# A hybrid decoder layer on one core: attention probabilities turned by VectorE blocks and a trip through DRAM

## What is computed

```python
scores = jnp.einsum('bnqchd,bnkchd->bnchqk', qb, kb,
                    preferred_element_type=jnp.float32) * (hd ** -0.5)
...
m = jnp.max(scores, axis=-1, keepdims=True)
e = jnp.exp(scores - m)
den = jnp.sum(e, axis=-1)
o = jnp.einsum('bnchqk,bnkchd->bnqchd', e, vb.astype(jnp.float32))
```

## Time and profile before

| | |
|---|---|
| time, three runs | 1344.31, 1344.43, 1344.99 us |
| span of the profiled execution | 1342.2 us |
| TensorE busy | 1331.9 us, 99% of the span |
| VectorE, ScalarE, GpSimd busy | 781.2, 507.8, 531.0 us |
| attention steps | about 328 to 850 us |

### The profile page before, as it was taken

One profiled execution on the slowest core, in us unless ns is written; L12 is line 12 of the kernel. 1 busy time (PEld: TensorE's weight loads), 2 busy tenths in 40 slices (PEclk: granted clock), 3 DMA queues, 4 the chain that ended last, 5 costly groups with the idle time before them and its releaser, 6 DMA issues.

```text
span 1342.2 us, 17647 instructions
## 1 busy us (share of the span) xinstructions
PE 1331.9 (99%) x6262; PEld 1104.3 (82%) x6262; DVE 781.2 (58%) x1253; ACT 507.8 (38%) x1282; POOL 531.0 (40%) x500
## 2 busy tenths in 40 slices
PE   9999999999999999999999999999999999999998
PEld 6887888888888888888888888888888888888887
DVE  6799887842779666565665752148512566134323
ACT  7455646542434444344443688311200011223100
POOL 6975424404458334041340632342067317044020
PEclk9999999999999999999999999999999999999999
DMA  6232312322203032120320332376279644122111
GB/s 240 79 102 87 109 56 79 110 100 72 75 12 84 24 92 64 31 83 22 97 58 30 114 98 88 100 237 220 94 275 412 198 126 157 55 79 63 40 47 47
DMA packets 84823, 139.51 MB, mean 104 GB/s; under 512 B 10464, under 2 KB 41472, under 8 KB 84736
## 3 DMA queue, kind: packets, MB, share of 16 engines
q10 hardware_dynamic: 40288, 75.82, 16.0%
q1 hardware_dynamic: 44448, 62.56, 15.6%
HBM read 108.84 MB, written 29.51 MB: 103 GB/s over the span
## 4 chain that ended last, share of the span: by engine, by line
PE 92%; DVE 5%; issue 1%; ACT 1%; DMA 0%; POOL 0%; SPq 0%; POOLq 0%; DVEq 0%; ACTq 0%
PE bank L1275 28%; PE bank L1280 28%; PE bank L1279 28%; PE bank L1432 2%; PE bank L1412 2%; PE bank L1399 1%; PE bank L1421 1%; DVE xc L1012 1%; PE bank L1525 1%; PE bank L1320 0%; DMA gain_mix<-in_gain_mix 0%; ACT L750 0%; DVE ibuf L1039 0%; DVE qkr L1116 0%; DVE ibuf L1028 0%
## 5 line engine op out<-in xcount | busy, mean ns | idle before, releaser
L549 POOL TENSOR_TENSOR ring<-raw,ring 128x512 fp32r<-128x512 f32 x221 | 310.5, 1405 | 727.1 <-PE bank L1280 642.8
L1275 PE MATMUL bank<-hn,ring 128*128 128x512 f32 x640 | 251.8, 393 | 1.4 <-DVE sgbuf L1000 1.2
L1280 PE MATMUL bank<-hn,ring 128*128 128x512 f32 x640 | 249.4, 390 | 0.0
L1279 PE MATMUL bank<-hn,ring 128*128 128x512 f32 x640 | 249.2, 389 | 0.0
L1275 PE MATMUL bank<-ring,hn 128*128 128x512 f32 x576 | 232.6, 404 | 0.2 <-POOL ring L549 0.2
L1280 PE MATMUL bank<-ring,hn 128*128 128x512 f32 x576 | 225.8, 392 | 0.0
L1279 PE MATMUL bank<-ring,hn 128*128 128x512 f32 x576 | 225.2, 391 | 0.0
L553 POOL TENSOR_SCALAR ring<-raw 128x512 fp32r<-128x512 f32 x221 | 183.5, 830 | 7.9 <-DMA raw<-in_w_rnn_s 7.8
L1275 PEld LDWEIGHTS bank<-hn,ring 128*128 128x128 f32 x640 | 120.2, 188 | 26.7 <-DVE sgbuf L1000 1.6
L1280 PEld LDWEIGHTS bank<-hn,ring 128*128 128x128 f32 x640 | 120.1, 188 | 25.3
L1279 PEld LDWEIGHTS bank<-hn,ring 128*128 128x128 f32 x640 | 120.3, 188 | 24.0
(11 more groups left out here) (181 smaller groups left out, 2153.7 us busy)
## 6 DMA issues: line engine op xcount, KB each, us to landing
raw<-in_w_tail_s SPq DMA_DIRECT2D x104, 256.0 KB, 2.7
g_in<-gate_dram ACTq DMA_DIRECT2D x48, 256.0 KB, 4.4
raw<-in_w_rnn_s SPq DMA_DIRECT2D x45, 256.0 KB, 2.6
raw<-in_w_qkv_s SPq DMA_DIRECT2D x48, 192.0 KB, 2.5
gate_dram<-g_out ACTq DMA_DIRECT2D x32, 256.0 KB, 2.1
raw<-in_w_qkv_s SPq DMA_DIRECT2D x48, 128.0 KB, 2.2
o_dram<-o_buf ACTq DMA_DIRECT2D x48, 128.0 KB, 1.8
o_in<-o_dram ACTq DMA_DIRECT2D x12, 512.0 KB, 3.5
```

The lines of the kernel that those rows point to most:

```text
L549: nc.gpsimd.tensor_tensor(ring[:, ring_slot(p), 1], raw[:, p % RAW], ring[:, ring_slot(p), 0].bitcast(F32), ALU.subtract).then_inc(w_ready, 1)
L1275: ins = T.matmul(out, lhs[0], rhs[0], start=first, stop=False)
L1279: T.matmul(out, lhs[0], rhs[1], start=False, stop=False)
L1280: return T.matmul(out, lhs[1], rhs[0], start=False, stop=last)
```

## The change

TensorE no longer turns the exponentials. VectorE turns each 32x32 block of the tile within itself, in place in `scores`. ScalarE's queue then writes the tile to a DRAM scratch tensor with four DMAs, one for each 32 partitions, in pieces of 32 numbers (128 B), and in the next step reads it back with one DMA, laid out so that the blocks stand in their turned places in `probsT`. Bank 6 and ScalarE's copy out of it are no longer used. The read takes a step of its own, so the product with the values comes one step later (lag 7), and there are 103 steps instead of 102.

```diff
-LAG_T, LAG_QK, LAG_ET, LAG_PV = 2, 4, 5, 6
+LAG_T, LAG_QK, LAG_ET, LAG_IN, LAG_PV = 2, 4, 5, 6, 7
...
+        turn_dram = nc.dram_tensor("turn_dram", (4, 2 * QUADS, QUAD, QUADS, QUAD), F32, kind="Internal").ap()
...
@@ ScalarE, attention(A), behind the copy to qkT
+                g = A - LAG_ET
+                if 0 <= g < TILES:
+                    b0 = 0 if has_prev(g // (HEADS * NT), g % NT) else QUADS
+                    act.wait_ge(et_done, g + 1)
+                    if g >= 4:
+                        act.wait_ge(probsT_in[g % 2], 16 * ((g - 4) // 2 + 1))
+                    for i in range(QUADS):
+                        act.dma_start(turn_dram[g % 4, b0:, :, i].rearrange("b i j -> i b j"),
+                                      scores[i * QUAD:(i + 1) * QUAD, g % 2, b0 * QUAD:].rearrange(
+                                          "p (b j) -> p b j", j=QUAD)).then_inc(et_out[g % 2], 16)
                 g = A - LAG_QK
...
@@ ScalarE, behind the exponential
-                g = A - LAG_ET
+                g = A - LAG_IN
                 if 0 <= g < TILES:
-                    act.wait_ge(et_done, g + 1)
+                    b0 = 0 if has_prev(g // (HEADS * NT), g % NT) else QUADS
+                    act.wait_ge(et_out[g % 2], 16 * QUADS * (g // 2 + 1))
                     if g >= 2:
                         act.wait_ge(pv_done, g - 1)
-                    nc.scalar.activation(probsT[:, g % 2, c0:], bank[6][:, c0:2 * P], ACT.Copy).then_inc(etc_done, 1)
+                    act.dma_start(probsT[:, g % 2, b0 * QUAD:].rearrange("p (b q) -> p b q", q=P),
+                                  turn_dram[g % 4, b0:].rearrange("(b c) i a j -> (c i) b (a j)", c=QUADS)
+                                  ).then_inc(probsT_in[g % 2], 16)
...
@@ VectorE, attention(A)
+                g = A - LAG_ET
+                if 0 <= g < TILES:
+                    c0 = 0 if has_prev(g // (HEADS * NT), g % NT) else P
+                    dve.wait_ge(exp_done, g + 1)
+                    V.transpose(scores[:, g % 2, c0:], scores[:, g % 2, c0:]).then_inc(et_done, 1)
                 g = A - LAG_QK
...
                     if g >= 2:
-                        dve.wait_ge(et_done, g - 1)
+                        dve.wait_ge(et_out[g % 2], 16 * QUADS * (g // 2))
...
@@ TensorE, attention(A)
-                g = A - LAG_ET
-                if 0 <= g < TILES:
-                    pe.wait_ge(exp_done, g + 1)
-                    if g >= 1:
-                        pe.wait_ge(etc_done, g)
-                    for b in ((0, 1) if has_prev(grp, tile) else (1,)):
-                        ins = T.transpose(bank[6][:, b * P:(b + 1) * P], scores[:, g % 2, b * P:(b + 1) * P], ident[:])
-                    ins.then_inc(et_done, 1)
...
-                    pe.wait_ge(etc_done, g + 1)
+                    pe.wait_ge(probsT_in[g % 2], 16 * (g // 2 + 1))
```

More of the change, by code:

```diff
@@ L35 @@
 CLASSES = (1, 4, 8)
+QUAD = 32
+QUADS = P // QUAD
 OFF_Z_RNN = RNN
@@ L402, in build_layer @@
         et_done = sem("et_done")
-        etc_done = sem("etc_done")
+        et_out = [sem("et_out0"), sem("et_out1")]
+        probsT_in = [sem("probsT_in0"), sem("probsT_in1")]
         pv_done = sem("pv_done")
@@ L752, in attention @@
                                          ).then_inc(exp_done, 1)
-                g = A - LAG_ET
+                g = A - LAG_IN
                 if 0 <= g < TILES:
-                    grp, tile = g // (HEADS * NT), g % NT
-                    c0 = 0 if has_prev(grp, tile) else P
-                    act.wait_ge(et_done, g + 1)
+                    b0 = 0 if has_prev(g // (HEADS * NT), g % NT) else QUADS
+                    act.wait_ge(et_out[g % 2], 16 * QUADS * (g // 2 + 1))
                     if g >= 2:
                         act.wait_ge(pv_done, g - 1)
-                    nc.scalar.activation(probsT[:, g % 2, c0:], bank[6][:, c0:2 * P], ACT.Copy).then_inc(etc_done, 1)
+                    act.dma_start(probsT[:, g % 2, b0 * QUAD:].rearrange("p (b q) -> p b q", q=P),
+                                  turn_dram[g % 4, b0:].rearrange("(b c) i a j -> (c i) b (a j)", c=QUADS)
+                                  ).then_inc(probsT_in[g % 2], 16)
                 g = A - LAG_PV
```

## The result

The changed kernel takes 1382.12 us (median of 4 runs, 1378.71 to 1384.34) against 1344.71 us (4 runs, 1344.31 to 1345.31): 1.0276 times the time before, with an interval of [1.0261, 1.0291]. 1345.0 with a range of 1338 to 1376 was predicted: the time is 37 us above the value and outside the range. The profiled span is 1376.9 us, 34.7 more than before.

The account below looks back on a forecast made before the run. TensorE, busy for 99% of the span, was taken to bound the kernel. -14.4 + 1.5 + 13.4 = +0.5 us on the profiled 1342.2, plus 2.2 from span to median, gave 1345 us, range 1338 to 1376.

Parts of the forecast that it names:

- The transposes removed: Qkv stage: 121 transposes at 0.11 us leave TensorE, 13.3 us, plus a 1.1 us wait: 14.4 us gained.
- The block transpose on VectorE: Every tile's step: 0.26 us for one block, 0.39 to 0.51 for two, hidden behind VectorE's idle time, costed at nothing.
- The price of an issue: ScalarE's queue: each write holds it 0.385 us (one-block tile) or 0.42 us (two-block tile), set between traced issues by piece count.
- The first rival: Issues are dear: at 0.50 us each the gate stage gets 7 us more, 1352, up to 1360 at 0.6; chance 0.25.
- So it is a microsecond early, and nothing waits: Qkv stage, two-block step: the read tile lands at 4.9 us, TensorE wants it at 5.9, so no wait.
- The chunk's end: Qkv stage: read 2 us later at chunk ends; three right before a step cost TensorE 0.5 us each, 1.5 us.
- The gate stage: ScalarE nearly full: 3.6 us more for each four steps, 14.4 over 16 steps, less about 1: 13.4 us lost.
- the three write steps behind these 16 have less work on ScalarE and cost nothing: Gate stage, after the last copy to `qkT`: ScalarE has less to do, so these steps add nothing.
- Late landing: Many small pieces make reads land 4 us after issue, TensorE waits 38 us in the steps: 1383; chance 0.12.
- ScalarE keeps up: Gate stage: an issue holds the queue only 0.28 us, so its loss is 8 us less 1: 1338.5; chance 0.20.
- The clock: Gate stage: waits make TensorE's clock fall, matmuls take twice as long, 66 us more, 14 hidden: about 1397; chance 0.03.
- The rule on short pieces: Writes in 128 B pieces: under 512 B DMA misses its rate; twice the traced 2 us would give Late landing's sum.

Follow-up runs that it names:

- e14: Changed kernel, writes put behind the exponential; round trip only for tiles 26 to 77 less those read at chunk ends, others turned on TensorE: 1338.02 us.
- e11: Changed kernel, writes behind the exponential, read ahead of it, two output banks; last 18 tiles turned on TensorE: 1345.77 us.
- e7: Changed kernel with each of the four writes cut in two (eight of 16 partitions, same 128 B pieces): 1473.79 us.
- e8: Changed kernel with four writes, but each row sent as one piece of 512 or 1,024 B, blocks left in wrong places: 1378.45 us.
- e4: Changed kernel, but the value product reads `ident` instead of the turned probabilities and doesn't wait for the read to land: 1364.82 us.
- e10: Changed kernel with the round trip for the first 78 tiles; the last 18 turned on TensorE and copied by ScalarE as before: 1355.09 us.
- e12: As e11, but the first 26 tiles too turned on TensorE; round trip only for tiles 26 to 77: 1340.65 us.

## Why the prediction was wrong

**The transposes removed: right.** 13.3 us at 0.11 each were taken off the qkv stage. In e14, where 43 tiles make the round trip and 62 transposes are gone (6.8 us), the time is 6.3 us shorter, with 0.8 us of waits for `o_buf`.

**The block transpose on VectorE: right in its price, wrong in "costs nothing".** It takes 0.31 us for one block and 0.43 for two, inside the bounds. But in the sentence "it hides behind that idle time" the average over 422 us stood for every step. In the two stretches in which GpSimd permutes, VectorE's rotations take three times as long (1.2 to 1.3 us against 0.42) and the transpose comes 1 to 5 us later in its step. What is behind it was not asked either: ScalarE's queue stands at the writes. That these stretches are what the first 26 tiles lose 5.1 us by is read from the trace and from e11 to e14, which take those tiles out as a whole; moving the permutation itself wasn't tried.

**The price of an issue: mis-sized.** 0.385 and 0.42 us were taken; the median is 0.455, and behind the first the issues in a row start 0.47 to 0.50 apart on either queue. The two of `cossin` were the right row, and the eight small ones the wrong one. "128 pieces, between these ends" assumed that pieces set the price; e7 and e8 show that between 32 and 256 pieces they hardly do. Why those eight came at 0.36 each stays open. The first rival had the price right, and its time (1352 to 1360) wrong, because it charged it to the gate stage alone.

**"So it is a microsecond early, and nothing waits": the step that failed in the qkv stage.** For a plain two-block step it held: of the 76 value products up to the gate stage 15 waited, nearly all at chunk ends or where GpSimd permutes. The landing times of the earlier trace rows spread from 1.8 to 4.4 us, and one number was taken for all steps. The median read lands in 2.1 us (2.2 was taken), but at chunk ends, beside weight loads and the bias load, most take 3 to 4. The chunk's end was seen, and priced 1.5 us; of the 19.4 us of waits up to 763 us, 13.6 lie there, 4.5 where GpSimd permutes, and one of 1.3 behind a read whose issue alone took 1.43 us. Summed from start to start of TensorE's matmuls in the qkv stage of the two traces, 13.1 us of transposes and 1.8 us of waits went, and 22.5 us of waits, 1.8 us in products whose weights were no longer loaded ahead, and 1.7 us of large matmuls, nearly all at the lower clock, came: +11.1, against +10.5 measured.

**The gate stage: the right mechanism, 10.8 us short.** Up to step 97 it lost 16.9 us where 13.4 were forecast. By the sum four steps were to take 19.57 + 3.6 = 23.2 us (the 22.5 named as a sign does not follow from that sum); they took 24.3 at first and 25.1 to 25.2 later. Of the 1.1 to 2.0 us missing, 4 x (1.80 - 1.54) = 1.0 are the issues' price. In the later steps some 0.6 are the landing (e4, without it, takes 24.4 to 24.5 there), and the rest is that not all of the 0.9 us taken as free could be used (in e4 ScalarE still waits 0.78 us for TensorE in each four steps). And "the three write steps behind these 16 have less work on ScalarE and cost nothing" was wrong: 7.3 us are lost behind step 97. There the writes still hold the queue for 1.8 us and more a step, now with no copy running beside them:

```profile
876.14 1.86 ACTq L755 DMA_DIRECT2D turn_dram<-scores  x4
...
878.54 0.28 ACT L782 ACTIVATE o_buf<-bank 128x128 f32<-128x128 f32 x1 [2.87 <-issue]
```

**The rivals.** Late landing came closest in time (1383) and for the wrong reason: it was priced as 0.3 to 0.75 us in every step, where it is 1 to 3 us in a few. "ScalarE keeps up" is out. The clock fell at two places (0.66 from 595 to 600 us; 0.90 and 0.76 in the two stretches of 5 us from 835), so the lower level held for about 3.4 us at each, and the gate stage as a whole didn't go to 1.2 GHz. The rule on short pieces (the Trainium skill, DMA: Bandwidth & Descriptors, Specifications) did not decide here: the writes in 128 B pieces land in 1.7 us, those in 512 and 1,024 B pieces in 1.6 (e8).

**Where the time lies.** From the changed kernel (1382.1) down to e14 (1338.0), each by a run: 27.0 us the gate stage, where ScalarE is full (to e10); 9.3 us the order of ScalarE's queue in the qkv stage (to e11); 5.1 us the first 26 tiles (to e12); 2.6 us the chunk ends (to e14). That is 44 us: the 37.4 us that the change lost, and the 6.3 that a round trip kept to quiet steps wins. Open is how the 5.1 us divide between the permutation and the filling of the first steps; what makes the reads at chunk ends late (weight loads, the bias load in the same queue, or VectorE); and how the waits would stand if SyncE issued at a better place.

## What to carry to other kernels

A DMA issue is an instruction of its queue: here near half a microsecond each in a row, with 32 pieces or 256 (eight small ones took 0.36 each). Ask what stands behind it in that queue and put it behind something long that already runs. Price a chain of hand-overs at its worst step (a chunk's end full of loads, a slow stretch of another engine), not at the average. And when a wait goes away and another of the same size takes its place, the engine that both come from is late, and only less work or another order on it helps.

## What the runs showed of the hardware

Of a group of four writes the second issue starts 0.35 us behind the first, and the others 0.47 to 0.50 us apart, on ScalarE's and SyncE's queue alike, with 32 pieces or 256. A DMA issue runs beside a table load or an activation that stands ahead of it (issue at 803.76, in the table load of 803.61 to 804.89), not beside one behind it (the table load of 803.61 stands 1.55 us idle behind four issues). Waits of 2.93 and 2.67 us of TensorE were each followed by eight large matmuls 0.42 to 0.52 us apart and by a granted clock of 0.66, and of 0.90 and 0.76, in the stretches concerned; behind a wait of 2.63 us (789.17) and the shorter ones it stayed at 1.00, so the length of the wait alone doesn't tell. Behind a wait the first matmul of a value product takes 0.21 us to the next instead of 0.11; its weights were not loaded ahead (the load starts with the matmul, at 596.31). VectorE's TENSOR_TENSOR operations of 128x256 take 1.2 to 1.3 us instead of 0.42 while GpSimd permutes `hn`. At chunk ends too they take up to 1.55: in the changed kernel's trace 79 of the 288 rotations take over 0.7 us, and GpSimd is busy for 90% of their time, against 5% of the others'.
